# A two-layer hybrid decoder trunk on one core: the first layer's second value block split by halves of its rows, rotary angles computed on GpSimd, and four idle products in a wait of TensorE

## The reference, cut to what matters

```python
def rope_tables(positions, dim):
    inv = ROPE_THETA ** (-jnp.arange(0, dim, 2, dtype=jnp.float32) / dim)
    ang = positions.astype(jnp.float32)[..., None] * inv
    return jnp.cos(ang), jnp.sin(ang)

def reference(x, c, positions, ...):
    cos_r, sin_r = rope_tables(positions, RET_DK)      # 64: retention heads
    cos_m, sin_m = rope_tables(positions, MLA_ROPE)    # 32: latent attention
    c_act = jax.nn.silu(c)
    for l in range(DEPTH):                             # 2 layers
        mod = c_act @ ada_w[l] + ada_b[l]
        sh_m, sc_m, g_m, sh_f, sc_f, g_f = jnp.split(mod, 6, axis=-1)
        h = modulate(rmsnorm(x, mix_pre_g[l]), sh_m, sc_m)
        t = h @ w_in[l]        # 1024 -> lru_x lru_g ret_q ret_k ret_v ret_g mla_cq mla_ckv mla_kr gates
        ...                    # three mixers, each to D_MODEL, merged by gates, @ w_out
        x = x + g_m[:, None, :] * rmsnorm(y, mix_post_g[l])
        h = modulate(rmsnorm(x, ffn_pre_g[l]), sh_f, sc_f)
        y = conv_glu(h, ...)   # 1024 -> 2 x 2816 -> 1024
        x = x + g_f[:, None, :] * rmsnorm(y, ffn_post_g[l])
    return x
```

## Time and profile before

| what | us |
|---|---|
| three runs, median (lowest, highest) | 934.29 (932.42, 935.62) |
| the profiled execution's own time | 934.45 |
| its span, first to last instruction | 932.6 |
| PE busy in the span | 909.3 |
| DVE busy | 731.4 |
| ACT busy | 535.4 |
| POOL busy | 86.2 |

### The profile page before, as it was taken

One profiled execution on the slowest core, in us unless ns is written; L12 is line 12 of the kernel. 1 busy time (PEld: TensorE's weight loads), 2 busy tenths in 40 slices (PEclk: granted clock), 3 DMA queues, 4 the chain that ended last, 5 costly groups with the idle time before them and its releaser, 6 DMA issues.

```text
span 932.6 us, 16982 instructions
## 1 busy us (share of the span) xinstructions
PE 909.3 (98%) x6752; PEld 853.8 (92%) x6752; DVE 731.4 (78%) x988; ACT 535.4 (57%) x715; POOL 86.2 (9%) x162
## 2 busy tenths in 40 slices
PE   6899999999999999999999999999999999999997
PEld 5799999999978999999979999999998799999996
DVE  4889888888787887886886887898789686666765
ACT  4456866555358555554673585954555764555554
POOL 0122202000001020000001220200000100000000
PEclk9799999999999999999999999999999999999999
DMA  9889867666883677776645986867668365556451
GB/s 363 295 258 311 278 220 247 226 204 213 326 284 110 221 257 256 258 245 203 197 147 168 256 292 205 267 200 262 217 221 298 106 221 186 180 184 212 137 188 46
DMA packets 135132, 209.06 MB, mean 224 GB/s; under 512 B 5536, under 2 KB 104224, under 8 KB 135072
## 3 DMA queue, kind: packets, MB, share of 16 engines
q1 hardware_dynamic: 120960, 162.73, 53.1%
q0 software_dynamic: 13824, 45.36, 13.5%
q10 hardware_dynamic: 288, 0.14, 0.0%
HBM read 204.28 MB, written 1.05 MB: 220 GB/s over the span
## 4 chain that ended last, share of the span: by engine, by line
PE 85%; DVE 5%; ACT 4%; DMA 3%; issue 2%; DVEq 0%; ACTq 0%; SPq 0%
PE banks L1808 79%; DVE w_lo L1168 2%; DMA raw<-in_w_in 2%; ACT w_hi L640 1%; PE banks L2079 1%; DMA adw<-in_ada_rows 1%; PE banks L1929 1%; DMA cst<-shape_constants 1%; PE banks L2086 1%; PE banks L1948 1%; DVE EF L1710 1%; PE banks L2095 1%; DVE adw L1161 1%; ACT h_hi L698 0%; ACT AB L867 0%
## 5 line engine op out<-in xcount | busy, mean ns | idle before, releaser
L1808 PE MATMUL banks<-h_lo,w_hi 128*128 128x256 f32 x1504 | 423.5, 282 | 2.1 <-DVE h_lo L1229 2.1
L1808 PE MATMUL banks<-h_hi,w_lo 128*128 128x256 f32 x1504 | 419.9, 279 | 0.0
L1808 PE MATMUL banks<-h_hi,w_hi 128*128 128x256 f32 x1504 | 419.8, 279 | 0.0
L1808 PEld LDWEIGHTS banks<-h_lo,w_hi 128*128 128x128 f32 x1504 | 282.6, 188 | 5.8 <-issue 4.3
L1808 PEld LDWEIGHTS banks<-h_hi,w_lo 128*128 128x128 f32 x1504 | 282.7, 188 | 0.9
L1808 PEld LDWEIGHTS banks<-h_hi,w_hi 128*128 128x128 f32 x1504 | 282.6, 188 | 0.0
L1168 DVE TENSOR_TENSOR w_lo<-raw,w_hi 128x2048 fp32r<-128x2048 f32 x96 | 219.5, 2288 | 32.2 <-ACT w_hi L640 31.2
L640 ACT ACTIVATE w_hi<-raw 128x2048 fp32r<-128x2048 f32 x96 | 182.6, 1911 | 97.6 <-PE banks L1808 77.3
L1710 DVE SCALAR_TENSOR_TENSOR EF<-banks,par,EF 128x254 f32<-128x254 f32 (+1 forms) x176 | 76.8, 477 | 57.3 <-ACT EF L1020 52.5
L1734 DVE TENSOR_TENSOR w_lo<-raw,w_hi 128x2048 fp32r<-128x2048 f32 x42 | 96.0, 2285 | 21.5 <-ACT w_hi L1039 21.5
L1039 ACT ACTIVATE w_hi<-raw 128x2048 fp32r<-128x2048 f32 x42 | 80.3, 1913 | 36.7 <-PE banks L1808 36.7
(11 more groups left out here) (281 smaller groups left out, 1238.7 us busy)
## 6 DMA issues: line engine op xcount, KB each, us to landing
raw<-in_w_in SPq DMA_DIRECT2D x52, 1024.0 KB, 6.7
raw<-in_ffn_w_up SPq DMA_DIRECT2D x44, 1024.0 KB, 5.0
adw<-in_ada_rows POOLq DMA_DIRECT2D x80, 512.0 KB, 5.6
raw<-in_ffn_w_down SPq DMA_DIRECT2D x22, 1024.0 KB, 4.9
raw<-in_w_out SPq DMA_DIRECT2D x8, 1024.0 KB, 8.3
raw<-in_ret_wo SPq DMA_DIRECT2D x4, 1024.0 KB, 6.0
raw<-in_lru_wo SPq DMA_DIRECT2D x4, 1024.0 KB, 5.1
raw<-in_mla_wo SPq DMA_DIRECT2D x4, 1024.0 KB, 7.3
```

Source lines behind the costliest of these rows:

```text
L1808: ins = MM(ps, lhs, rhs, start=first and n == 0, stop=last and n == 2)
```

## The change

Four edits, all in the first layer's start:

1. Block 1 is split by halves of its rows. ScalarE makes `w_hi` of columns 0 to 1023 of the slot first, then modulates and splits h for chunk 0, then makes the other half, then does chunk 1. VectorE makes `w_lo` in two halves, with `h_low` of chunk 0 between. In `v_product(0, 1)` TensorE waits for the first half at the start and for the second before its third group of rows.
2. `angles` and the cast move from VectorE to GpSimd, which has them behind the wait for the positions. [...] The transfers of the recurrence gates stand between the two calls; the rotations come behind the second.
3. Four idle products (`keep_going(0, 4)`) stand between `v_product(1, 0)` and `v_product(0, 1)`. Their result is never read.
4. Two semaphores are used twice (`sig_c` becomes `c_sig_v1_hi`, `c_ready` becomes `c_v1_lo`), for the two events of the first half.

```diff
@@ GpSimd
+            def next_to(ins):
+                steps[0] += 1
+                ins.then_inc(pool_step, 1)
+                pool.wait_ge(pool_step, steps[0])
+            def angles(s, c, inv):
+                next_to(V.tensor_scalar(s[:], rs2[:, 0], inv, None, ALU.mult))
+                next_to(V.tensor_scalar(rs2[:, 1], s[:], 1.0 / TWO_PI, MAGIC, ALU.mult, ALU.add))
+                next_to(V.tensor_scalar(rs2[:, 1], rs2[:, 1], MAGIC, None, ALU.subtract))
+                for part_2pi in (*PARTS, REST):
+                    next_to(V.tensor_scalar(c[:], rs2[:, 1], -part_2pi, None, ALU.mult))
+                    next_to(V.tensor_tensor(s[:], s[:], c[:], ALU.add))
+                next_to(V.tensor_scalar(c[:], s[:], PI / 2, TWO_PI, ALU.is_gt, ALU.mult))
+                next_to(V.tensor_scalar(rs2[:, 1], s[:], TWO_PI / 4, None, ALU.add))
+                next_to(V.tensor_tensor(c[:], rs2[:, 1], c[:], ALU.subtract))
+                next_to(V.tensor_scalar(c[:], c[:], PI, -PI, ALU.min, ALU.max))
+                V.tensor_scalar(s[:], s[:], PI, -PI, ALU.min, ALU.max).then_inc(ang_ready, 1)
+            pool.wait_ge(pos_in, 16)
+            next_to(V.tensor_copy(rs2[:, 0], pos_i))
+            angles(sinr, cosr, inv_ret)
             pool.wait_ge(hi_ready.s, hi_ready.at(0, 3))
             recurrence_weights(0)
+            angles(sinm, cosm, inv_mla)
@@ ScalarE
-            split_block(0, 1)
+            act.wait_ge(*landed(0, 1))
+            A_(w_hi[:, at_slot(0, 1), 0:D], raw[:, at_slot(0, 1), 0:D], ACT.Copy).then_inc(c_sig_v1_hi, 1)
             act.wait_ge(mod_ready.s, 1)
             modulate(0, 0, 0, 1)
+            h_high(0, 0, 0, 1)
+            A_(w_hi[:, at_slot(0, 1), D:2 * D], raw[:, at_slot(0, 1), D:2 * D], ACT.Copy).then_inc(hi_ready.s, 1)
             modulate(0, 1, 1, 1)
-            h_high(0, 0, 0, 1)
             h_high(0, 1, 1, 1)
             split_block(0, 2)
@@ VectorE
-            split_block(0, 1)
+            dve.wait_ge(c_sig_v1_hi, 2)
+            s1 = at_slot(0, 1)
+            V.tensor_tensor(w_lo[:, s1, 0:D], raw[:, s1, 0:D], w_hi[:, s1, 0:D].bitcast(F32), ALU.subtract).then_inc(c_v1_lo, 1)
             h_low(0, 0, 0, 1)
+            split_lo(0, 1, w_lo[:, s1, D:2 * D], raw[:, s1, D:2 * D], w_hi[:, s1, D:2 * D].bitcast(F32))
             h_low(0, 1, 1, 1)
             split_block(0, 2)
...
-                    dve.wait_ge(pos_in, 16)
-                    step(V.tensor_copy(rs2[:, 0], pos_i))
-                    angles(sinr, cosr, inv_ret)
...
-                    angles(sinm, cosm, inv_mla)
@@ TensorE
-                    ready(l, j)
+                    by_halves = l == 0 and (c, i) == (0, 1)
+                    if by_halves:
+                        pe.wait_ge(c_v1_lo, 2)
+                    else:
+                        ready(l, j)
...
+                        if by_halves and k == 2:
+                            ready(l, j)
...
                 if l == 0:
                     v_product(1, 0)
+                    keep_going(0, 4)
                     v_product(0, 1)
```

More of the change, by code:

```diff
@@ L302, in trunk_kernel @@
         mod0_evac, mod0_ready = sem("mod0_evac"), sem("mod0_ready")
-        sig_c, c_ready, pro = sem("sig_c"), sem("c_ready"), sem("pro_dve")
+        c_sig_v1_hi, c_v1_lo, pro = sem("c_sig_v1_hi"), sem("c_v1_lo"), sem("pro_dve")
         st_zero = sem("st_zero")
+        pool_step = sem("pool_step")
         ang_ready, trig_ready = sem("ang_ready"), sem("trig_ready")
@@ L539, in recurrence_weights @@
                         pool.dma_start(wbd[64 * b:64 * b + 64, m, :, 64 * b:64 * b + 64], blockw).then_inc(wbd_in.s, 16)
+            V = nc.gpsimd
+            steps = [0]
+            def next_to(ins):
+                steps[0] += 1
+                ins.then_inc(pool_step, 1)
+                pool.wait_ge(pool_step, steps[0])
+            PI = 3.1415925
+            TWO_PI = 6.283185307179586
+            PARTS = (6.28125, 2029 / 2 ** 20)
+            REST = TWO_PI - PARTS[0] - PARTS[1]
+            MAGIC = 12582912.0
+            def angles(s, c, inv):
[13 more added lines that the diff above has]
+            angles(sinr, cosr, inv_ret)
             pool.wait_ge(hi_ready.s, hi_ready.at(0, 3))
             recurrence_weights(0)
+            angles(sinm, cosm, inv_mla)
             def next_tiles(first, last):
@@ L604, in _ @@
             act.wait_ge(c_in, 16)
-            A_(ccol[:, 1, :], ccol[:, 0, :], ACT.Sigmoid).then_inc(sig_c, 1)
-            act.wait_ge(sig_c, 1)
+            A_(ccol[:, 1, :], ccol[:, 0, :], ACT.Sigmoid).then_inc(c_sig_v1_hi, 1)
+            act.wait_ge(c_sig_v1_hi, 1)
             A_(pbuf[:, 1, 376:384], ccol[:, 1, :], ACT.Sqrt)
@@ L1096, in step @@
                 dve.wait_ge(pro, st_n[0])
[L1099 to L1120, removed]
+            dve.wait_ge(c_sig_v1_hi, 1)
+            V.tensor_tensor(ccol[:, 2, :], ccol[:, 0, :], ccol[:, 1, :], ALU.mult).then_inc(c_v1_lo, 1)
             def softplus(stage):
@@ L1870, in first_modulation @@
                 ins.then_inc(ada0_used, 1)
-            pe.wait_ge(c_ready, 1)
+            pe.wait_ge(c_v1_lo, 1)
             for k in range(DK):
```

## The result

| kernel | median (lowest, highest) of 5 runs, us | profiled execution: own time, span |
|---|---|---|
| before | 934.29 (932.42, 935.62) | 934.45, 932.6 |
| after | 942.25 (941.62, 942.35) | 942.29, 940.5 |

The ratio is 1.0091 with a 95% interval of 1.0078 to 1.0103: the change costs 8 us. The forecast, 933.7 with a range to 938.6, was wrong.

A forecast was written before the change was run, and what follows sets the result against it. TensorE was taken as the bound, busy 909.3 of 932.6 us. Halves net of idle products -0.62 and angles 0 took 934.45 to 933.8, or 933.7 from the median 934.29; range 932.0 to 938.6.

The forecast's parts named there:

- Mean step 0.58: Angles on GpSimd: 29 steps at a mean of 0.58 us, so the second call is done at 56.6.
- the free time: Lateness of the second angle call that costs TensorE nothing: an end up to 64.7, 1.9 us late.
- the rival's own sum: GpSimd cannot read SBUF during VectorE's w_lo: second call done at 67.7, net +2.4 us, 936.8; chance 0.28.
- at 0.7 it is +6: Within the exclusion rival: a mean GpSimd step of 0.7 us would make the change cost 6 us.
- From 64.7 on, one for one: Second angle call ending past 64.7 delays w_lo of blocks 7 to 9; TensorE loses each further us.
- The rotations are covered: Rotations behind the second angle call cost nothing, as VectorE wants the first only past 67.1.
- The move gives nothing: TensorE has no hole there to close: Angles moved from VectorE to GpSimd: on time with 7 and 6 us of slack, effect 0.
- The step that checked the slack of block 2's `w_lo`: Block 2's w_lo ends near 42.8 and TensorE wants it at 43.8: 1 us of slack.
- Gain 0.62: Block 1 by halves, with idle products: product (0,1) starts at 38.10 instead of 38.72, gaining 0.62 us.
- They cost 0.9, earn 0: Four idle products before (0,1) take 0.9 us of the halves' gain; the clock does not fall there.
- rival on the clock: Clock may fall in the wait before block 1; idle products prevent it, winning up to 2 to 4 us; 0.08.

The follow-up runs named there:

- e5: The kernel after, with an idle second operation (add 0.0) given to the one-operation tensor_scalar instructions of both angle calls on GpSimd; 940.16 us, ratio 1.0059.
- e8: The kernel after, with the transfers of the first two rotations issued by ScalarE ahead of the second pair of sines; 941.86 us, ratio 1.0095.
- e6: e1 with the cast and first angle call on VectorE placed behind w_lo of block 3 instead of ahead of it; 932.52 us, ratio 0.9995.
- e1: The kernel after, with the angles and cast back on VectorE in their old places, halves and idle products kept; 933.72 us, ratio 1.0003.
- e2: The kernel before, with only the angles moved to GpSimd as in the kernel after; 942.29 us, ratio 1.0090.
- e4: The kernel after, with the second angle call back on VectorE behind w_lo of block 5, the first still on GpSimd; 935.50 us, ratio 1.0023.
- p_write: The kernel before, with 12 extra GpSimd memsets of 128x896 on a scratch tile from the landing of the positions on; 936.87 us in one execution.
- e3: e1 without the four idle products; 934.94 us, ratio 1.0011.
- e7: e6 without the four idle products; 932.27 us, ratio 0.9992.
- p_read: The kernel before, with 12 extra GpSimd instructions of 128x256 reading a scratch tile from the landing of the positions on; 934.7 us in one execution.
- p_occupied: The kernel before, with extra GpSimd instructions reading a scratch tile, 15 ahead of the gates' transfers and 17 behind them; 948.59 us, ratio 1.0154.
- p_occupied_short: The kernel before, with extra GpSimd instructions reading a scratch tile, 15 ahead of the gates' transfers and 11 behind them; 944.20 us, ratio 1.0116.

## Why the prediction was wrong, by its steps

**"Mean step 0.58" failed, on both of its halves.** It put one-input instructions at 0.45; they took 0.85 with one operation (0.94 where the factor is read from a tile: L559 at 56.05 in e5), 0.40 with multiply and add or with minimum and maximum, and 1.09 with a comparison. Two inputs took 0.74, predicted 0.64 by halving the 1.27 of 512 columns: a part of some 0.2 us does not halve. Without stretches the 29 steps come to 0.83 each, semaphore included: some 7.1 us more than predicted. The exclusion, which the forecast put at nothing, adds some 10.5. Together 17.6, and the second call ended at 74.3 in place of 56.6. Neither would have given the whole: at 0.83 without exclusion it ends near 64, just inside the free time; at 0.58 with it the rival's own sum gave 67.7 and 936.8. That rival had the mechanism and the place right; its price was too low by the length of the steps, for longer steps meet more `w_lo`. Its text had the warning ("at 0.7 it is +6").

**"From 64.7 on, one for one" held for VectorE's path**, in after and in e5. Put into it, the end that was measured gives 934.3 + 9.6 - 0.6 = 943.3 against 942.25. It is not all of the price: from e5's own before, 933.52 + 5.2 - 0.6 = 938.1 against 940.16, of which 1.2 is the lower clock, a term that the sum lacked. (TensorE wanted block 9 at 83.73, not 83.9, so 0.6 and not 0.8 was free there.)

**"The rotations are covered" failed**, unseen in after, since the sines hide it: e8 and the two occupied runs show that VectorE wants the first at about 71, and it came 3.4 us behind the call in after (landed at 77.67), 3.8 in the occupied runs and 6.6 in e5. The step had a lower bound for when VectorE wants it, 67.1, and no sum at all for when it lands.

**"The move gives nothing: TensorE has no hole there to close" failed.** There was no hole in before, but no slack at block 3 either. The step that checked the slack of block 2's `w_lo` did not go on to block 3's, behind 4.3 us of angles. The move does give room there: in after `w_lo` of block 3 ends at 46.06 and TensorE takes the block at 50.59. e6 gives the same room without GpSimd.

**"Gain 0.62" was mis-sized**: in e1 the product (0,1) starts at 37.61 in place of 38.10 and block 2 gains 1.01. In after's own execution block 0 began 2.05 us later (29.88 for 27.83): the sixteen one-column products at 16.4, for instance, took 3.41 us in place of 2.09. So (1,0) ended at 37.66 and the idle products (1.54 us at clock 1.00) pushed (0,1) to 39.20, and block 2 starts 0.58 later than in before, not 0.62 sooner. That slower head stands in the profiled executions of e2, e4, e5, e8 and p_write too, and not in the others; what brings it about no run tells. In after it costs nothing, as VectorE sets block 9's time.

**"They cost 0.9, earn 0" failed in the kernel that has the wait at block 3**: by the medians e3 is 1.2 us slower than e1, not 0.9 faster. It held where that wait is gone, to within what e6 and e7 tell apart. The prediction's rival on the clock has cases of its own, in two executions whose head is that of before: p_read and p_occupied. TensorE waits 2.6 and 2.7 us there before block 1 (2.3 in before), and behind this wait the granted clock is 0.50 from 39.8 to 43.2; block 2 starts 1.4 us later than in before. The window of p_read:

```profile
39.90:42.70 2.80, 2.80 (x8) 2.20 (x7) 2.76 (x3) 1.91 (x1) 2.72 (x2) 0.50 0.01 3
```

Before has 13 products and 1.00 in this stretch. Whether four idle products prevent such a fall no pair of runs tested.

## What to carry to other kernels

Work moved to an idle engine is priced by that engine's own steps and by what shares its port: list each two-input SBUF instruction of VectorE beside it, and add them before asking whether it is on time. A queue that is moved delays everything behind it, and a deadline for a transfer is the landing, not the issue. When a gain at the head is forecast, walk it forward block by block until a slack is smaller than the gain; the next instruction in that queue is the one to move first.

## What the runs showed of the hardware

- On GpSimd a `tensor_scalar` of 128x256 float32 with one operation took 0.85 us, with multiply and add 0.40: adding a second, idle operation made the multiplication faster (L563 in e5: 0.41). An addition did not gain: L567 with a second addition took 1.08 in place of 0.86. The subtraction with an addition (L561 in e5) was beside a `w_lo` both times, 3.00 and 3.07 us, and ended 0.94 behind it, where in after it had ended 0.72 behind: it did not gain either.
- A GpSimd instruction that reads SBUF was held up to 2.1 us by VectorE's subtraction of two SBUF tensors (p_read, 2.91 for 0.85); one that only writes was not (p_write, 0.85 to 0.88).
- GpSimd memsets stretched three of VectorE's one-input instructions, which take 0.35, 0.46 and 0.29 in before, to 0.90 each (p_write).
- The granted clock was at its lower level, 0.50, from 75.5 to 82.3 in after, where TensorE had stood from 73.1 to 79.2, and from 50.5 to 53.9 in e3 behind a wait of 1.84 us; behind the one of 1.06 us in e1 it was 1.00. Where VectorE's queue set TensorE's pace anyway, as in after, the lower clock cost nothing; in e3 it cost 1.5 us, in e5 (0.50 from 83.8 to 87.2) 1.2 us, in p_read (0.50 from 39.8 to 43.2) 1.4 us at block 2 and in p_occupied_short (0.50 from 81.9 to 92.2) 1.8 us.
